# Four dot products of gathered rows moved from the rounds to the stretch ahead of them, in a one-core attention, gating and product-key block

## The reference, cut to what matters

```python
q = (xt @ w_query).reshape(T, 8, 2, 128)
s = einsum('thpd,hpnd->thpn', q, sub_keys)            # scores against 128 keys on each side
...                                                   # top 16 of the sums, ids and softmax gates
def block(args):                                      # 128 tokens each, 8 * 16 = 128 picks per token
    xb, idb, gb = args
    a = einsum('tkd,td->tk', expert_down[idb], xb)
    act = gelu(a) * gb
    return einsum('tk,tkd->td', act, expert_up[idb])
```

## Time and profile before

| | us |
|---|---|
| median of three runs | 1464.06 |
| the profiled execution, its own time | 1463.16 |
| its span, first to last instruction | 1461.3 |
| PE busy | 1420.1 (97%) |
| DVE busy | 1183.7 (81%) |
| ACT busy | 667.6 (46%) |
| POOL busy | 562.5 (38%) |
| bytes moved by DMA | 407.03 MB, mean 279 GB/s |

### The profile page before, as it was taken

One profiled execution on the slowest core, in us unless ns is written; L12 is line 12 of the kernel. 1 busy time (PEld: TensorE's weight loads), 2 busy tenths in 40 slices (PEclk: granted clock), 3 DMA queues, 4 the chain that ended last, 5 costly groups with the idle time before them and its releaser, 6 DMA issues.

```text
span 1461.3 us, 21875 instructions
## 1 busy us (share of the span) xinstructions
PE 1420.1 (97%) x7662; PEld 1279.3 (88%) x7662; DVE 1183.7 (81%) x2465; ACT 667.6 (46%) x1085; POOL 562.5 (38%) x458
## 2 busy tenths in 40 slices
PE   3999999999999899999999999999999999999998
PEld 3787789999999899999988888888888888888887
DVE  6987975678888888899678787878788888888887
ACT  3566553444445666777533333333333333333334
POOL 0000001264454458888533343433344344344440
PEclk9999999999999999999999999999999999999999
DMA  9965433455554477787899989999999899999994
GB/s 347 387 216 194 160 106 120 129 197 180 172 179 140 147 253 267 272 295 258 332 370 369 369 313 388 340 353 340 334 329 380 316 374 346 343 373 360 318 330 145
DMA packets 187710, 407.03 MB, mean 279 GB/s; under 512 B 13192, under 2 KB 100816, under 8 KB 185936
## 3 DMA queue, kind: packets, MB, share of 16 engines
q1 hardware_dynamic: 148016, 245.96, 48.6%
q0 software_dynamic: 36864, 134.23, 25.0%
q10 hardware_dynamic: 2720, 25.44, 4.7%
HBM read 362.59 MB, written 42.99 MB: 278 GB/s over the span
## 4 chain that ended last, share of the span: by engine, by line
PE 89%; DVE 4%; ACT 2%; SPq 1%; issue 1%; POOL 1%; DMA 1%; DVEq 0%; ACTq 0%; POOLq 0%
PE bank L2069 12%; PE bank L2071 12%; PE bank L2070 12%; PE bank L1996 11%; PE bank L1998 11%; PE bank L1997 11%; PE bank L2051 5%; PE bank L1965 2%; PE bank L1966 2%; PE bank L1964 2%; SPq L536 1%; PE bank L1986 1%; DMA w_in_sb<-in_w_in 1%; DVE part L1231 1%; PE bank L1848 1%
## 5 line engine op out<-in xcount | busy, mean ns | idle before, releaser
L1996 PE MATMUL bank<-h2hi,dhi 128*128 128x384 f32 x1024 | 346.6, 338 | 4.2 <-DVE dlo L1440 4.1
L1998 PE MATMUL bank<-h2hi,dlo 128*128 128x384 f32 x1024 | 343.2, 335 | 0.0
L1997 PE MATMUL bank<-h2lo,dhi 128*128 128x384 f32 x1024 | 342.8, 335 | 0.0
L2069 PE MATMUL bank<-uhi,ahi 128*128 128x512 f32 x768 | 298.8, 389 | 0.0
L2070 PE MATMUL bank<-ulo,ahi 128*128 128x512 f32 x768 | 298.8, 389 | 0.0
L2071 PE MATMUL bank<-uhi,alo 128*128 128x512 f32 x768 | 298.7, 389 | 0.0
L1440 DVE TENSOR_TENSOR dlo<-down,dhi 128x1024 fp32r<-128x1024 f32 x128 | 161.8, 1265 | 159.8 <-ACT dhi L961 159.8
L739 POOL DMA_INDIRECT rows<-in_peer_up,ids x128 | 162.9, 1273 | 236.7 <-DVE y L1524 206.9
L739 POOL DMA_INDIRECT rows<-in_peer_down,ids x128 | 163.2, 1275 | 215.7 <-DVE rows L1515 197.0
L961 ACT ACTIVATE dhi<-down 128x1024 fp32r<-128x1024 f32 x128 | 135.1, 1056 | 206.3 <-PE bank L1998 205.9
L1996 PEld LDWEIGHTS bank<-h2hi,dhi 128*128 128x128 f32 x1024 | 192.4, 188 | 8.9 <-DVE dlo L1440 5.9
(11 more groups left out here) (249 smaller groups left out, 2079.1 us busy)
## 6 DMA issues: line engine op xcount, KB each, us to landing
down<-in_down_t SPq DMA_DIRECT2D x128, 512.0 KB, 5.4
up<-in_peer_up SPq DMA_DIRECT2D x128, 512.0 KB, 7.5
ada<-in_w_ada SPq DMA_DIRECT2D x48, 512.0 KB, 10.4
gate<-gates_dram SPq DMA_DIRECT2D x32, 768.0 KB, 11.9
gates_dram<-stage ACTq DMA_DIRECT2D x11, 2048.0 KB, 7.2
gel_dram<-gel SPq DMA_DIRECT2D x80, 192.0 KB, 3.4
gelu<-gel_dram SPq DMA_DIRECT2D x80, 192.0 KB, 6.5
wq<-in_peer_query SPq DMA_DIRECT2D x16, 512.0 KB, 5.3
```

Of the source, the lines that this page charges most:

```text
L1996: pe.matmul(bank[7 * s][:, 0:TD], dhi[s][:, k, :], h2hi[:, k, 0:TD], start=k == 0, stop=False)
L1997: pe.matmul(bank[7 * s][:, 0:TD], dhi[s][:, k, :], h2lo[:, k, 0:TD], start=False, stop=False)
L1998: last = pe.matmul(bank[7 * s][:, 0:TD], dlo[s][:, k, :], h2hi[:, k, 0:TD], start=False, stop=k == KT - 1)
L2069: pe.matmul(got[:], ahi[j][:, tokens], uhi[j][:, half], start=first, stop=False)
```

## The change

The stretch between gates and rounds gets four dots, one behind the low part of each of down tiles 76 to 79. A new constant DOTS_AFTER = 4 goes into DOTS_EARLY, which rises from 31 to 35. So dots 31 to 34 are done there, in buffers 0 to 3, and the rounds begin with dot 35. `rows_by_step` spreads 93 dots over the first 72 steps of PLAN (97 over 74 before) and the 128 additions into `y` over 99 steps (97 before).

```diff
-DOTS_HEAD, DOTS_PICKS, DOTS_TURNS = 3, 3, 16
+DOTS_HEAD, DOTS_PICKS, DOTS_TURNS, DOTS_AFTER = 3, 3, 16, 4
 FIRST_DOTS = 3
 DOTS_ROUTING = DOTS_HEAD * (PH - 1 - FIRST_DOTS) + DOTS_PICKS
-DOTS_EARLY = DOTS_ROUTING + DOTS_TURNS
-assert DOTS_TURNS % ROWS_KEPT == 0
+DOTS_EARLY = DOTS_ROUTING + DOTS_TURNS + DOTS_AFTER
+assert DOTS_TURNS % ROWS_KEPT == 0 and DOTS_AFTER % ROWS_KEPT == 0
...
             for n in range(AFTER_G, EARLY + 2):
                 down_lo(n, n % 2)
+                if n - AFTER_G < DOTS_AFTER:
+                    row_op(DOTS_EARLY - DOTS_AFTER + n - AFTER_G)
                 if 2 <= n - AFTER_G < 2 + AHEAD:
                     up_lo(n - AFTER_G - 2)
```

## The result

The changed kernel took 1468.81 us (median of 14 runs, 1467.33 to 1476.32) against 1463.96 us (14 runs, 1462.42 to 1468.02) for the kernel before: a ratio of 1.0038, 95% interval 1.0029 to 1.0047. I had forecast +3.1 us and called it the same; it is +4.9 us, slower, and clear of the noise. It lies just over the 0.3% (4.4 us) that the prediction took as its line, and the interval reaches down to that line. The time is inside the stated range, whose top was 1469.2. In a later session the changed kernel gave 1470.27 against 1465.06 us, ratio 1.0036 (1.0020 to 1.0053).

The account below looks back on a forecast made before the run. PE, busy 97% of the span and full from 704 us on, was taken as the bound. Rounds 0, DVE in the stretch 0 and gates +3.1 us on 1464.06 gave 1467.2, rounded to 1467.0 us; range 1463.6 to 1469.2.

Parts of the forecast that it names:

- Rounds give back 0: In the rounds DVE has 4.9 us less to do, but PE waits for nothing there: 0 us.
- DVE in the stretch, 0: Between gates and rounds, four dots of 1.22 us fit in DVE's gaps and the low parts keep their time: 0 us.
- x = 4.3 us from three gathers at 1.43: Ahead of the rounds, three of four extra gathers pass before the gates' first load, making the gates 4.3 us late.
- Cover 1.15 us: At the fourth up, DVE's product is ready at 752.00 and PE wants it at 753.15: 1.15 us of lateness covered.
- What PE loses is x - 1.15, and no more: At the first four ups, PE loses the gates' lateness less 1.15 us of cover, for good: 3.1 us.
- The same, 0.77: Whole kernel: 1467.0 us, 0.2% more, within the 0.3% (4.4 us) that counts as no change; chance 0.77.
- rival 2: Ahead of the rounds, all extra gathers pass before the gates, 4.6 us and more: 1468.6 us and up; chance 0.20.

Follow-up runs that it names:

- two gathers: The kernel before with two gathers added into unused buffers, behind the low parts of tiles 77 and 78: 1465.83 against 1465.06 us, ratio 1.0010.
- DVE late: The kernel before with six unread products put on DVE ahead of its first multiplication by the gates: 1469.34 against 1465.06 us, ratio 1.0028.
- PE kept busy: The changed kernel with 19 matmuls added on PE ahead of the first up: 1467.48 us against 1463.55 for the kernel before, ratio 1.0030.

## Why the prediction was right and wrong, point by point

- *Rounds give back 0.* Right: no PE wait was there to be shortened, and none changed but the first.
- *DVE in the stretch, 0.* Right, to the hundredth: the low parts of tiles 77 to 79 and 81 keep their distance from the last turn. Only tile 80's was 0.56 us later (738.35 less 8.01, against 729.78), because its load came late, inside its cover of 1.6 us.
- *x = 4.3 us from three gathers at 1.43.* Measured 4.89, with all four ahead. Shared out over four that is 1.22 each, below my 1.43; the variants gave 1.28 to 1.40. I had let row 40 pass behind the gates because it was issued when they were. It went ahead: it was in at 747.7 us and DVE had the gates only at 750.55, 11.41 us after their issue, 7.08 before. The Trainium skill's rule on turns between queues, weighed in the prediction (DMA: Bandwidth & Descriptors, "Queues, rings and completion order"), would have had all four pass first, and the traces agree: queue 0 took 29% and queue 1 lost 25.5 points of its share (102.7% to 77.2%).
- *Cover 1.15 us.* The other cover bound. The gap came at the first up, with 1.5 us (4.89 - 3.39, and the same 1.50 with two gathers and with DVE late). At the fourth up, where 1.15 us would have counted, PE was itself 1.8 us later by then, through its slow first up; with PE kept busy, and so with no slow up, the fourth up did bind. So the stall of 3.39 us was met within 0.3 us by 3.1 by luck, with two errors against each other: x 0.6 us too low and the cover 0.35 too small.
- *What PE loses is x - 1.15, and no more.* This is the step that failed. I priced a PE gap at its length. With the measured x it gives 4.89 - 1.15 = 3.74 us, and 5.15 were lost. Behind the gap the granted clock was 0.64 over 4.7 us, which added 1.76 us, half as much again as the gap: 3.39 + 1.76 = 5.15 where I had 3.1. DVE's lateness alone did the same, 3.48 + 1.72. With PE kept busy the clock stayed at 1.00, and the loss was 4.59 us where x - 1.15 gives 5.17 - 1.15 = 4.02. So of the 1.4 us beyond my formula some 0.8 are the clock's own and 0.6 are small distances at later ups that I had left out. The Trainium skill (TensorE: Matmul & The Clock Gate, "Part 1: The HAM clock gate") says that TensorE's clock goes back to its half after PE has stood idle; I did not weigh it, though the forecast itself made a gap. I had looked only at PE behind 704 us, which had none; the trace of before has one of 2.54 us at 479.31 (clock 1.00 behind it) and one of 2.16 us at 40.00 (0.64 behind it). The penalty is not in proportion to the gap, and not certain: behind idle times of 0.2, 0.9 and 1.95 us the clock stayed at 1.00, behind the 2.54 us near 479 us it fell in four traces of twelve, behind 2.29 us in the one case in the rounds, and behind 3.2 to 3.9 us in all four.
- *The same, 0.77.* Wrong by that term: with it the sum is 1464.0 + 5.2, over the 0.3% bound. The bounds of my range had the same hole: I took the greatest stall as the greatest loss. That the median, 1468.8, still lies under the top of 1469.2 shows nothing for the mechanism. My rival 2 put slower at 0.20 on all four gathers passing, which is what happened.

What stays open: why the turns of the gates take from 182 to 190 us. POOL's own instructions ahead of the turns' matmuls are what PE waits for (the row of 718.78), 6.0 us in six waits in the changed kernel's first trace and 0.9 us in one wait before. The longest of POOL's 96 instructions of L786 takes 3.27 us in the six traces whose turns are over 184 us, the kernel before with four added gathers among them, and 2.62 in the six others. What lengthens them was not tried. Open too is why the clock falls behind the same gap in some executions only.

## What to carry to other kernels

A step moved off a full engine's neighbour is free on that neighbour and still not free: it frees buffers, and what these start (here four gathers of 512 KB, each of which made the next load 1.2 to 1.4 us later) joins a queue that may have no air. Add up the bytes that must land before the next point at which the bound engine waits, and look at the DMA share there, before the compute. And price a gap in a busy TensorE not at its length alone: the slow matmuls behind gaps of 3.2 us and more took 1.7 to 1.8 us on top here, and there were none behind gaps under 2 us. What that costs in the end depends on who is late: here keeping PE busy through the gap gave back only 0.6 to 0.8 of the 1.76 us, since DVE, not PE, was behind.

## What the runs showed of the hardware that I had not expected

After 3.2 us of idle time of PE the matmuls of 512 columns started 0.43 us apart instead of 0.227, some 8 of them, with the granted clock back at 1.00 after that. After idle times of 0.2, 0.9 and 1.95 us the clock of the stretch behind read 1.00; after 2.29 and 3.2 us it read 0.64 over some 4.7 us. It is no matter of the length alone: the same wait of 2.54 us near 479 us, in the same code, was followed by 1.00 in eight traces and by 0.64 or 0.65 in four, and cost 1.5 us more in those. So executions of one program can differ by 1.5 us with nothing changed. Queue 0's gathers, few and of 4 KB rows, took 29% of the 16 engines' time from queue 1 with its packets of 512 bytes (77.2% where it had 102.7%), though the gates' loads were issued before the last of them.
